# GpSimd in place of VectorE for the first feed-forward's modulation products, and one 512-column pass for rounded weights

## What is computed

```
ada = silu(c) @ w_ada + b_ada                      # 9 vectors of 1024: sh1, sc1, g1, ... g3
h = rmsnorm(x, ffn1_norm) * (1 + sc1) + sh1
x = x + 0.5 * g1 * ((silu(g) * u) @ ffn1_w_out)    # g, u = split(h @ ffn1_w_in)
```

## Time and profile before

| | |
|---|---|
| median of 3 runs | 1501.88 us |
| lowest, highest | 1498.55, 1507.09 us |
| the profiled execution | 1498.06 us, span 1495.7 us |
| TensorE busy | 1445.4 us (97% of the span) |
| VectorE, ScalarE, GpSimd busy | 632.6, 444.1, 27.6 us |
| mean granted TensorE clock | 0.991 |

### The profile page before, as it was taken

The page is one execution under the profiler, slowest core; times in us unless marked ns, Lnnn a source line. Parts: engine busy times, 40 slices in busy tenths (PEclk is TensorE's granted clock), DMA queues, the critical chain, the costliest instruction groups (busy, mean ns, idle before and its releaser), DMA issues.

```text
span 1495.7 us, 23349 instructions
## 1 busy us (share of the span) xinstructions
PE 1445.4 (97%) x9898; PEld 1017.4 (68%) x9898; DVE 632.6 (42%) x1037; ACT 444.1 (30%) x679; POOL 27.6 (2%) x36
## 2 busy tenths in 40 slices
PE   6999999999999999999999989999999999999997
PEld 3976854444444444444344449999999778999997
DVE  5786240111100011011001019888878676655555
ACT  3434031111111111111111125344344354455453
POOL 0011000000000000000000000000020000000000
PEclk9999999999999999999999999999999999999999
DMA  9959799999999999999999995888767730455551
GB/s 359 358 210 346 288 383 426 430 432 427 428 430 431 426 430 429 427 429 431 429 427 432 429 391 206 308 310 306 247 232 281 261 113 30 155 169 199 194 168 56
DMA packets 117426, 481.00 MB, mean 322 GB/s; under 512 B 12108, under 2 KB 59465, under 8 KB 96769
## 3 DMA queue, kind: packets, MB, share of 16 engines
q1 hardware_dynamic: 115936, 476.46, 80.9%
q0 software_dynamic: 736, 2.31, 0.5%
q10 hardware_dynamic: 705, 1.51, 0.3%
HBM read 479.20 MB, written 1.06 MB: 321 GB/s over the span
## 4 chain that ended last, share of the span: by engine, by line
PE 73%; DMA 21%; DVE 2%; ACT 2%; issue 1%; SPq 0%; DVEq 0%; ACTq 0%
DMA arena<-in_w_up_dram 18%; PE psum L1584 14%; PE psum L1724 8%; PE psum L1790 7%; PE psum L1606 6%; PE psum L1702 6%; PE psum L1697 5%; PE psum L1222 3%; PE psum L1710 3%; PE psum L1692 3%; PE psum L1346 3%; PE psum L1565 2%; PE psum L1547 2%; DMA arena<-in_w_in_dram 2%; DMA arena<-in_ffn_w_in_dram 1%; PE psum L1228 1%
## 5 line engine op out<-in xcount | busy, mean ns | idle before, releaser
L1584 PE MATMUL psum<-arena,squares 128*64 128x384 f32 x2048 | 339.3, 489 | 20.6 <-DMA arena<-in_w_up_dram 11.8
L1584 PEld LDWEIGHTS psum<-arena,squares 128*64 128x64 f32 x2048 | 146.4, 137 | 215.8 <-issue 186.1
L2319 DVE TENSOR_TENSOR mixT<-mixT,psum 128x384 f32<-128x384 f32 x32 | 26.5, 828 | 496.3 <-PE psum L1584 496.3
L1606 PE MATMUL psum<-arena,small 128*64 128x512 f32 x768 | 171.9, 596 | 0.0
L1606 PEld LDWEIGHTS psum<-arena,small 128*64 128x64 f32 x768 | 52.3, 137 | 96.2 <-issue 94.4
L2386 DVE TENSOR_TENSOR ff_w_lo<-arena,ff_w_hi 128x2048 fp32r<-128x2048 f32 x44 | 100.5, 2284 | 0.0
L1702 PE MATMUL psum<-ff_x_parts,ff_w_lo 128*128 128x256 f32 x704 | 91.5, 283 | 0.0
L1702 PEld LDWEIGHTS psum<-ff_x_parts,ff_w_lo 128*128 128x128 f32 x704 | 88.9, 192 | 1.6
L1028 ACT ACTIVATE ff_w_hi<-arena 128x2048 fp32r<-128x2048 f32 x44 | 83.9, 1907 | 0.2 <-DMA arena<-in_ffn_w_in_dram 0.2
L1697 PE MATMUL psum<-ff_x_parts,ff_w_hi 128*128 128x512 f32 x336 | 79.9, 390 | 0.0
L1000 ACT ACTIVATE small<-psum 128x384 f32<-128x384 f32 x32 | 15.7, 490 | 213.6 <-PE psum L1592 213.6
(11 more groups left out here) (352 smaller groups left out, 1956.6 us busy)
## 6 DMA issues: line engine op xcount, KB each, us to landing
arena<-in_w_gate_dram SPq DMA_DIRECT2D x32, 3072.0 KB, 33.2
arena<-in_w_up_dram SPq DMA_DIRECT2D x31, 3072.0 KB, 34.8
arena<-in_w_down_dram SPq DMA_DIRECT2D x31, 3072.0 KB, 32.1
arena<-in_ffn_w_in_dram SPq DMA_DIRECT2D x44, 1024.0 KB, 7.4
arena<-in_w_ada_dram SPq DMA_DIRECT2D x18, 2048.0 KB, 12.5
arena<-in_w_mod_dram SPq DMA_DIRECT2D x11, 2048.0 KB, 15.2
...
arena<-in_w_in_dram SPq DMA_DIRECT2D x10, 2048.0 KB, 9.4
```

Source lines behind the costliest of these rows:

```text
L1584: last = pe.matmul(b[64 * half:64 * half + 64, 0:HALF_E], lhsT=xeT[:, k, u * SLOTS:(u + 1) * SLOTS], rhs=w[:, k, half * HALF_E:(half + 1) ...
L1606: last = pe.matmul(bank[6][64 * half:64 * half + 64, :], lhsT=hiddenT[:, f % 3, 64 * (f // 3):64 * (f // 3) + 64], rhs=down[:, f, half * 5 ...
```

## The change

- **TensorE, ScalarE, VectorE:** the first feed-forward now takes the form of the second in every step but the first: one pass of 16 matmuls with 512 columns for w_hi, then the w_lo pass, with the two halves added by `sum_halves`. In step 1 the passes over ff_x_hi and ff_x_lo stay apart and go to different halves.
- **The product** silu(gate) x up reads up from gate_up_sum, in SBUF, and no longer from PSUM.
- **GpSimd** does the ten items. For each it forms the first product in mod_acc, then seven times a product in a buffer of its own (item_products, in mixT, which is free then) and adds it to mod_acc. Each operation waits for the one that it depends on, and item n + 1 waits for item n's transpose.
- **VectorE** keeps only `item_sums`, in steps j = 1 and j = 3 of a round, after act_rest.

The line numbers behind the first edit move: up to about L1697 they grow, and on VectorE they are six or more lower than before.

```diff
+        item_products = mixT[:, 0:4, :].rearrange("p (i a) t -> p i (a t)", i=2)
...
+            def mod_item(it, u):
+
+                w = ring(4 + u).rearrange("p (k n) -> p k n", k=KD)
+                pool.wait_ge(sem(f"ada_full{4 + u}"), it * 16 + 16)
+                for k in range(KD):
+                    if k == 0:
+                        nc.gpsimd.tensor_scalar(mod_acc[:, 0, :], w[:, 0, :], cond2[:, 0:1], 0.0, ALU.mult, ALU.add)\
+                          .then_inc(sem("mod_acc_step"), 1)
+                    else:
+                        product = item_products[:, k % 2, :]
+                        if k > 2:
+                            pool.wait_ge(sem("mod_acc_step"), it * 16 + 8 * (1 + u) + k - 1)
+                        step(nc.gpsimd.tensor_scalar(product, w[:, k, :], cond2[:, k:k + 1], 0.0, ALU.mult, ALU.add))
+                        pool.wait_ge(sem("mod_acc_step"), it * 16 + 8 * (1 + u) + k)
+                        nc.gpsimd.tensor_tensor(mod_acc[:, 0, :], mod_acc[:, 0, :], product, ALU.add)\
+                          .then_inc(sem("mod_acc_step"), 1)
+
+            for n in range(2 * FF_LOOPS):
+                if n:
+                    pool.wait_ge(sem("item_turned"), n)
+                mod_item(n // 2, n % 2)
...
-                    if key == "ffn1":
-                        nc.scalar.activation(gate_up_sum[:, parity, 0, :], bank[4 + 2 * parity][:, 0:T], ACT.Silu)\
-                          .then_inc(sem("ff_silu"), 1)
-                        return
                     if more:
-                        act.wait_ge(sem("ff_summed"), s - 1)
+                        act.wait_ge(sem("ff_summed"), s - 1 + past(key))
                     nc.scalar.activation(ff_b[:, :, :], psum[:, 4 + 2 * parity:6 + 2 * parity, T:2 * T], ACT.Copy)\
                       .then_inc(sem("ff_b_taken"), 1)
-                    act.wait_ge(sem("ff_summed"), s)
+                    act.wait_ge(sem("ff_summed"), s + past(key))
                     gate = gate_up_sum[:, parity, 0, :]
                     nc.scalar.activation(gate, gate, ACT.Silu).then_inc(sem("ff_silu"), 1)
...
                     pe.wait_ge(sem("ff_w_hi"), s + past(key))
-                    if taken is not None and key == "ffn1":
-                        pe.wait_ge(sem("ff_act"), taken)
-                    elif taken is not None:
-                        pe.wait_ge(sem("ff_summed"), taken)
+                    if taken is not None:
+                        pe.wait_ge(sem("ff_summed"), taken + past(key))
...
-                    elif key == "ffn1":
-                        for g in range(2):
-                            for k in range(KD):
                                 pe.matmul(to[g][:, 0:T], lhsT=w_hi[:, k, g, :], rhs=ff_x_hi[:, k, :], start=(k == 0), stop=False,
                                           skip_group_check=True)
                     else:
...
-                                             stop=(k == KD - 1 and key == "ffn2"), skip_group_check=True)
-                    if first or key == "ffn1":
-                        at = 0 if key == "ffn1" else T
+                                             stop=(k == KD - 1), skip_group_check=True)
+                    if first:
+                        at = T
                         for j in range(2 * KD):
-                            k, g = (j // 2, j % 2) if first else (j % KD, j // KD)
-                            if g == 0 and first:
+                            k, g = j // 2, j % 2
+                            if g == 0:
...
                 if ada_items:
-                    pe.wait_ge(sem("ff_act"), 4 * FF_LOOPS + 1)
+                    pe.wait_ge(sem("ff_summed"), 4 * FF_LOOPS + 1)
                     ada_columns(bank[4], 2 * FF_LOOPS, 0).then_inc(sem("ada_cols_ready"), 1)
                 down_by_bank(4 * FF_LOOPS + 2, 3, 1, 1)
...
 
-                    if key == "ffn1":
-                        return
-                    dve.wait_ge(sem("ff_b_taken"), s)
+                    dve.wait_ge(sem("ff_b_taken"), s + past(key))
                     nc.vector.tensor_tensor(gate_up_sum[:, parity, :, :], psum[:, 4 + 2 * parity:6 + 2 * parity, 0:T], ff_b[:, :, :],
...
-                    by = bank[5 + 2 * parity][:, 0:T] if key == "ffn1" else up
-                    nc.vector.tensor_tensor(up, gate_up_sum[:, parity, 0, :], by, ALU.mult).then_inc(sem("ff_act"), 1)
+                    nc.vector.tensor_tensor(up, gate_up_sum[:, parity, 0, :], up, ALU.mult).then_inc(sem("ff_act"), 1)
...
-                def mod_steps(it, lo, hi):
-
-                    for n in range(lo, hi):
-                        u, j = n // 8, n % 8
-                        w = ring(4 + u).rearrange("p (k n) -> p k n", k=KD)
-                        at = it * 16 + 8 * (1 + u)
-                        if j == 0:
-                            dve.wait_ge(sem(f"ada_full{4 + u}"), it * 16 + 16)
-                            i = nc.vector.tensor_scalar(mod_acc[:, 0, :], w[:, 0, :], cond_2[0], None, ALU.mult)
-                        else:
-                            dve.wait_ge(sem("mod_acc_step"), at + j)
-                            i = nc.vector.scalar_tensor_tensor(out=mod_acc[:, 0, :], in0=w[:, j, :], scalar=cond_2[j],
-                                                               in1=mod_acc[:, 0, :], op0=ALU.mult, op1=ALU.add)
-                        i.then_inc(sem("mod_acc_step"), 1)
-                        if j == 7:
-                            item_sums(bass.ds(it * 32 + 16 * u, 16), it * 2 + u + 1)
...
-                        if with_ada:
-                            mod_steps(it, *((0, 5), (5, 9), (9, 13), (13, 16))[j])
+                        if with_ada and j % 2 == 1:
+                            u = j // 2
+                            item_sums(bass.ds(it * 32 + 16 * u, 16), it * 2 + u + 1)
```

17 lines of the change are left out of this document (removed).

## The result

The changed kernel takes **1561.81 us** (median of 3 runs, 1556.17 to 1565.85) against 1501.88 before: a ratio of **1.040**, 95% interval 1.037 to 1.0425. The forecast was 1562. The profiled execution took 1556.17 us, with a span of 1554.0.

A forecast was written before the change was run, and what follows sets the result against it. TensorE, busy 1445.4 of 1495.7 us, was taken as the bound. The last transpose coming 65 us later, less 1 us at the end, gave +64 us on 1498.06: 1562 us, range 1515 to 1600.

The forecast's parts named there:

- The ring: First feed-forward: GpSimd's item and VectorE's transpose wait on each other through one accumulator; 23.8 us per two steps, now 17.3.
- Item alone: GpSimd's 8 products and 7 additions for one item, undisturbed by VectorE: 16.3 us.
- Handover: GpSimd waits for VectorE's transpose and its signalling before the next item: 0.8 us per item.
- What they do to each other: VectorE operations with two SBUF inputs hold up GpSimd's reads: 6.7 us lost per item, bounds 5.1 and 8.7.
- the full sum, 8.7 us: Upper bound of GpSimd's loss per item, if each VectorE operation with two SBUF inputs costs its full length.
- Start: Item 0, from its weights' landing to the first transpose: at about 933 instead of 926.82.
- Loop: Nine more items at 23.8 us each: last transpose at 1147.2 instead of 1082.22, 65.0 us later.
- End: From the last transpose to the end of down_by_bank: about 8 us instead of 9.2, 1 us less.
- Signs: Expected trace marks: transposes 23.8 us apart, GpSimd's additions often over 2 us, TensorE idle about 62 us, 512-column passes 3.64 us.
- my last rival: TensorE's clock falls as it stands still in each item, making TensorE the bound: +153, 1651 us; chance 0.04.
- The rival "GpSimd keeps pace": First feed-forward: GpSimd and VectorE overlap, two steps take 17.1 us, no slowdown, 1496 us; chance 0.14.
- Half of it: Long operations share the port: GpSimd loses 3 us per item, not 6.7; +27, 1525 us; chance 0.08.

The follow-up runs named there:

- gpsimd_only: The kernel before with only the items moved to GpSimd, without the 512-column form: 1555.65 us, ratio 1.033.
- two_acc: The changed kernel with a second accumulator, so GpSimd starts an item without waiting for the transpose of the one before: 1545.53 us, ratio 1.029.
- double_rest: The changed kernel with VectorE forming ff_out_lo twice in each step of the first feed-forward: 1579.05 us, ratio 1.0505.
- triple_sum: The changed kernel with VectorE forming the sum of halves three times per step, one input in PSUM: 1559.06 us, ratio 1.037.
- memsets: The changed kernel with seven products and seven additions of each GpSimd item replaced by 14 memsets: 1498.44 us, ratio 0.998.
- form512_only: The kernel before with the 512-column form in the first feed-forward, all products still on VectorE: 1508.68 us, ratio 1.004.
- placed: The kernel before with the 512-column form, products on VectorE, one per step placed where VectorE waited for ScalarE's silu: 1498.72 us, ratio 0.998.

## Why the prediction was right

**The bound and the direction.** The ring GpSimd, transpose, ff_w_lo, TensorE was forecast and is what the waits show. gpsimd_only shows that it makes the slowdown by itself.

**Item alone: 16.3 forecast, 15.0 measured.** The addition takes 1.29 us, not 1.33; and the wait ahead of a product is for a semaphore that has long been given (the product's buffer came free one pair earlier), so 0.09 us of a wait were counted seven times for nothing: 7 x (1.42 - 1.27) = 1.05. The rest is the products' pitch, 0.78, and 0.67 for the first. By the Trainium skill, "GPSIMD Engine Reference", section "Performance versus the Vector engine", the estimate was 1.12 us; the trace shows 1.29, so the value scaled from two sizes of one kind was the nearer one.

**Handover: 0.8 forecast, 0.84 measured.** two_acc gains 1.0 per item without it.

**What they do to each other: 6.7 forecast, 6.8 in the item shown, 6.9 over ten.** Right in size and in kind (double_rest, triple_sum and memsets), though partly by two errors that cancel. I had counted only the time in which data pass, 2.12 us for ff_w_lo; a held product lost 2.29, the instruction's whole length (the product at 1004.55, which began with a ff_out_lo of 1.21, lost 1.05, so there its first 0.16 us were not lost). That is what the Trainium skill says in "SBUF — State Buffer", section "Who interferes with whom", and here the trace agrees with it against my reading. But not each of VectorE's eight instructions costs GpSimd: where they meet the other way round, VectorE is the one that waits, 0.70, 0.40, 1.09 and 1.10 us in the item shown. So the full sum, 8.7 us, was not reached.

**Start: near in number, wrong in its path.** The first transpose was forecast for 933, when GpSimd would be done with item 0, and came at 935.42. GpSimd began at 904.99, 2.3 us later than forecast, and its first product was held up for 4.3 us; yet it was done at 928.75, and the transpose came 6.7 us later without waiting for it. VectorE was the late one. The eight operations of the first block's last gain, which have two inputs in SBUF, took 9.12 us beside GpSimd's products and additions in place of 3.25 (the last row, of the kernel before):

```profile
904.99 4.99 POOL L776 TENSOR_SCALAR mod_acc<-arena,cond 128x512 f32<-128x512 f32 x1 [786.28 <-DMA arena<-in_w_ada_dram]
...
927.42 1.33 POOL L784 TENSOR_TENSOR mod_acc<-mod_acc,mixT 128x512 f32<-128x512 f32 x1
...
912.29 9.12 DVE L1991 SCALAR_TENSOR_TENSOR xT<-xT,cols_a,rstd 128x256 f32<-128x256 f32 x8
...
909.41 3.25 DVE L1997 SCALAR_TENSOR_TENSOR xT<-xT,cols_a,rstd 128x256 f32<-128x256 f32 x8
```

So it is luck that the start is off by only 2.4 us.

**Loop:** 9 x 22.62 = 203.6 in place of 214.2, 10.6 us less. **End:** forecast 1 us shorter, measured the same: the last row of down_by_bank ends at 1147.79 + 0.40 = 1148.19, 9.19 us behind the last transpose, 9.16 before. **Behind it** 1.3 us more than before. In sum +2.4 - 10.6 + 1.0 + 1.3 = -5.9, from 1562 to the profiled 1556.17. The median, 1561.81, is nearer to the forecast than the profiled execution is, by chance: against the median of before the forecast would have been 1566. The mis-sized term is the item alone.

**Signs.** Transposes 23.8 us apart: 22.6. VectorE released by GpSimd: yes. TensorE idle before ff_w_lo for 62 us: only 34.4, 6.9 of them ahead of the first transpose. 512-column passes of 3.64 us: yes, from start to start of the passes (933.90 and 937.54); the single row shows 3.80, as in the earlier trace rows. "The additions often over 2 us": wrong, the products were; which of the two is held depends on where they meet VectorE.

**Most of the missing idle time went into a lower clock**, the mechanism of my last rival in small. TensorE's busy time rose by 24.2 us, in spite of the shorter form. The item shown has it: the w_lo pass took 3.67 us behind the standstill, in place of 2.08, at a granted clock of 0.52.

```profile
1010.21 3.67 PE L1714 MATMUL psum<-ff_x_parts,ff_w_lo 128*128 128x256 f32 x16 [2.99 <-DVE ff_w_lo L2380]
...
935.42:1139.00 203.58, 176.14 (x1055) 161.40 (x1054) 128.01 (x110) 73.56 (x91) 190.72 (x135) 0.90 0.67 231
```

The second line is the window from the first transpose to the last: PE, PEld, DVE, ACT and POOL busy, then the granted clock, 0.90, so that part of the time was at 1.2 GHz. With a pitch of 22.62 TensorE has 9 x (22.62 - 16.87) = 51.8 us to spare in this window, not 62: 27.4 are standstill (203.58 - 176.14), and 24.3 went into the lower clock. It costs nothing while GpSimd is the bound and standstill is left over. The clock was back at 1.00 at once, from 1013.72 to 1016.60, and the next w_lo pass, at 1020.27, took 2.08 us again, so it never came to 1651.

**The rival "GpSimd keeps pace"** fails by the loss of 6.8 alone: undisturbed, item and handover would be 15.8 us, even better than the 17.1 I gave it, and under TensorE's 16.87; memsets, with 15.7, didn't bind. **"Half of it"** is refuted by the 2.29 and by double_rest.

**What the prediction didn't see** is a reason for the change: it priced the form's extra work on VectorE only with the products gone. form512_only shows that with them on VectorE the form loses 0.4%, and placed that the order of four operations mends it.
